# Adding the norms' squares on the vector engine before the ones-matmul

## The chip, the cores and the metric

The kernel runs on all eight cores of one Trainium2 chip. Each core computes one element of the batch by itself, with the same program and the same weights, and the cores exchange nothing. The time is that of the slowest core, in device microseconds (us). It is compared with the median of the runs of the kernel before.

## The reference

A trunk of two layers works on x (8, 2048, 1024). Each layer is: half-step SwiGLU FFN, token mixer, cross-attention into 256 memory tokens, half-step FFN. Every one of these eight sub-layers has an RMS norm ahead of it (pre-norm) and one behind it (post-norm):

```python
def rms_norm(x, g):
    xf = x.astype(jnp.float32)
    y = xf * lax.rsqrt(jnp.mean(xf * xf, axis=-1, keepdims=True) + EPS)
    return (y * g.astype(jnp.float32)).astype(x.dtype)

h = swiglu(rms_norm(x, g[0]), ...)
x = x + HALF * rms_norm(h, g[1])
h = rms_norm(x, g[2]); h = even_mixer(h, ...)   # layer 0; odd_mixer in layer 1
x = x + rms_norm(h, g[3])
h = cross_attention(rms_norm(x, g[4]), rms_norm(mem, mem_norm_g[l]), ...)
x = x + rms_norm(h, g[5])
h = swiglu(rms_norm(x, g[6]), ...)
x = x + HALF * rms_norm(h, g[7])
```

The mean runs over the 1024 channels. It is this sum of squares over the channels that the change is about.

## The kernel before

**Layout.** Channels lie on partitions: the 1024 channels are 8 chunks (c) of 128. The 2048 tokens are four blocks (tb) of 512, and a half (hf) is two blocks. X holds the residual stream (float32, 8 chunks by 2048 tokens), XN the normed input (bf16), HO the output of a sub-layer before its post-norm (float32, 8 chunks by the 1024 tokens of a half). HO2 is a second HO, used only by the second half of attention. Weights stream from memory through eight slots, issued on POOL.

**A group** is a run of matmuls into one bank of PSUM (8 banks, ps0 to ps7): 8 matmuls of 512 columns in a projection, 22 in the FFN's down projection. `k.bank()` hands out the banks in rotation and passes over those that are reserved.

**Sum over channels.** The chunks are summed over partitions by matmuls with a constant matrix (ONESM, all 1/1024), which add a chunk's squares over its 128 partitions and leave the sum on every partition. Two places do it:

- Post-norm, `HalfOut.evac(c, tb, bank)`: ACT copies the group's result, scaled by the gain, into HO (L577), squares the same bank into a small bf16 tile SQD (L580, three tiles in rotation), and two groups later PE takes that square through ONESM (`stat_mm`), eight matmuls for a block of tokens, into a bank kept reserved from chunk 0 on.
- Pre-norm, `prenorm_steps`: `sa` squares chunks 0 to 3 of X into SQP (one ACT instruction, L518), `sb_` takes them through ONESM in four matmuls and then squares chunks 4 to 7 into the same SQP (L525), `sc1` takes these through ONESM in four more, makes the reciprocal root on ACT (`rstd_from`, L463 and L465, an Ln and an Exp) and lets DVE write XN for chunks 0 to 3 (`xn_apply`, L531), `sc2` the same for 4 to 7.

**Order.** There is no scheduler: each engine executes its instructions in the order in which the Python code records them, and waits by semaphores on the keys of the tiles that it reads and writes. A key that another engine still has to read is waited for too. What belongs to a norm is recorded in between the groups of whatever follows: `run_seq(steps)` takes a list of (count, step), and a step is recorded once that many groups have gone by (`_tick`), or sooner, all steps up to it, when an operation outside the list needs a key that a step of the list writes or reads (`_check`), or when the next list begins (`need`). Before the change a ones-matmul of `evac` counts as a group too.

**After a half**, `finish` records such a list: the last ones-matmuls, then step A (or A2, two chunks of both blocks), in which DVE multiplies HO by the root (L620, L658) and DVE or POOL adds it to X (L622, L661), and then the pre-norm steps of the next sub-layer for these tokens. Behind the output projections of mixers and attention (`out_proj`), the evacuations are held back by three groups, and the second half's groups follow the first half's at once. There the list of the first half runs beside the groups of the second, and what is left of it is recorded in one go when the second half finishes; then the next sub-layer's first groups are recorded, which need all of XN of the first two blocks.

## Time and profile before

| | |
|---|---|
| median of 3 runs | 3073.16 us (3071.93 to 3591.28) |
| the profiled execution's own time | 3073.69 us |
| its span on the slowest core | 3072.1 us |
| PE busy | 2887.0 us (94%), 13124 matmuls |
| DVE busy | 1002.2 us (33%) |
| ACT busy | 1059.4 us (34%) |
| POOL busy | 627.8 us (20%) |
| spans of the eight cores | 3062.0 to 3072.1 us |
| mean granted TensorE clock of the cores | 0.970 to 0.973 |

The span goes from the first to the last instruction of the slowest core; 1.6 us of the execution lie outside it. Busy time is the union of an engine's instructions, and a busy PE may still be running at its lower clock, which is why the count of matmuls in a stretch says more than its busy share.

### The profile page before, as it was taken

The numbers are of one execution on the slowest core, as the hardware profiler recorded it, in microseconds if no ns is written. First come the engines' busy times: TensorE is split into PE (matmuls) and PEld (weight loads), VectorE is DVE, ScalarE is ACT, GpSimd is POOL, SyncE is SP. The second block draws the span as 40 slices with busy tenths as digits, with TensorE's granted clock in tenths as the row PEclk, the third lists the DMA queues.
The fourth block names the chain that finished last, engine by engine and source line by source line (L and its number), as shares of the span: only waits on it lengthen the run. The fifth ranks groups of instructions, "written<-read, shape, count | busy, mean of one in ns | idle before, by whom it ended". The sixth has DMA issues, their size and how long they took to land.

```text
span 3072.1 us, 38455 instructions; the slowest of 8 cores (3062.0 to 3072.1 us)
## 1 busy us (share of the span) xinstructions
PE 2887.0 (94%) x13124; PEld 1286.1 (42%) x13124; DVE 1002.2 (33%) x1485; ACT 1059.4 (34%) x1588; POOL 627.8 (20%) x966
## 2 busy tenths in 40 slices
PE   6999999889987889999999999998998898999997
PEld 2444444333333434444444444443443443444443
DVE  3212312242236336105105105205645427312212
ACT  4123213214764564124124124122126376213112
POOL 1114113110022122114112114112113204111121
PEclk9999999889998999999999999999999999999998
DMA  7554545353033434545555545554453622545667
GB/s 170 76 75 71 79 69 79 55 76 42 6 53 49 73 56 62 75 70 79 76 72 76 76 67 78 77 72 65 72 90 48 93 35 48 76 73 91 118 90 144
DMA packets 126173, 226.78 MB, mean 74 GB/s; under 512 B 13088, under 2 KB 24608, under 8 KB 125984
## 3 DMA queue, kind: packets, MB, share of 16 engines
q0 software_dynamic: 115376, 205.28, 45.2%
q1 hardware_dynamic: 10608, 19.03, 2.0%
q8 instruction: 112, 1.84, 0.3%
q14 instruction: 77, 0.63, 0.1%
HBM read 421.10 MB, written 8.39 MB: 140 GB/s over the span
## 4 chain that ended last, share of the span: by engine, by line
PE 81%; DVE 7%; ACT 6%; issue 3%; DMA 2%; POOL 0%; DVEq 0%; ACTq 0%; POOLq 0%; SPq 0%
PE ps L220 81%; DVE HO L620 3%; DVE XN L531 1%; DMA slot<-wflat 1%; DVE DG L797 1%; DVE X L622 1%; ACT sqp L525 1%; ACT RD L1163 0%; ACT ET L1151 0%; ACT RD L1164 0%; ACT r L463 0%; ACT L939 0%; ACT sqp L518 0%; ACT sqd L580 0%; ACT r L465 0%
## 5 line engine op out<-in xcount | busy, mean ns | idle before, releaser
L220 PE MATMUL ps<-XN,slot 128*128 128x512 bf16 x7296 | 1628.7, 384 | 45.0 <-DVE XN L531 31.7
L220 PEld LDWEIGHTS ps<-XN,slot 128*128 128x128 bf16 x7296 | 718.6, 99 | 944.5 <-issue 109.2
L321 POOL DMA_DIRECT2D slot<-wflat x800 | 425.0, 535 | 2255.9 <-PE ps L220 2216.1
L220 PE MATMUL ps<-H,slot 128*128 128x512 bf16 x2816 | 626.1, 379 | 1.5 <-DMA slot<-wflat 1.5
L748 DVE TENSOR_TENSOR H<-ps,s 128x512 bf16<-128x512 f32 x352 | 241.7, 690 | 1115.1 <-PE ps L220 1096.1
L739 ACT ACTIVATE s<-ps 128x512 f32<-128x512 f32 x352 | 209.3, 598 | 801.3 <-PE ps L220 733.9
L220 PEld LDWEIGHTS ps<-H,slot 128*128 128x128 bf16 x2816 | 275.2, 98 | 334.6 <-issue 3.6
L577 ACT ACTIVATE HO<-ps,cf_sb 128x512 f32<-128x512 f32 x256 | 176.5, 690 | 515.4 <-PE ps L220 507.9
L620 DVE TENSOR_TENSOR HO<-HO,r 128x512 f32<-128x512 f32 x192 | 194.4, 1037 | 97.4 <-ACT r L465 97.4
L531 DVE SCALAR_TENSOR_TENSOR XN<-X,cf_sb,r 128x512 bf16<-128x512 f32 x256 | 176.7, 758 | 137.6 <-ACT r L465 137.6
L622 POOL TENSOR_TENSOR X<-X,HO 128x512 f32<-128x512 f32 x104 | 153.8, 1504 | 106.7 <-DVE HO L620 102.3
L580 ACT ACTIVATE sqd<-ps 128x512 bf16<-128x512 f32 x256 | 152.4, 595 | 55.0 <-PE ps L220 55.0
L220 PE MATMUL ps<-sqp,onesm 128*128 128x512 bf16 x256 | 77.0, 430 | 55.9 <-ACT sqp L518 35.7
L220 PE MATMUL ps<-O,slot 128*128 128x512 bf16 x512 | 118.6, 379 | 0.2
L220 PE MATMUL ps<-CC,DG 128*128 128x512 bf16 x496 | 114.2, 389 | 0.0
L220 PE MATMUL ps<-sqd,onesm 128*128 128x512 bf16 (+1 forms) x272 | 97.2, 375 | 14.0 <-ACT sqd L580 14.0
L658 DVE TENSOR_TENSOR HO<-HO,r 128x512 f32<-128x512 f32 x64 | 44.9, 735 | 132.2 <-ACT r L465 132.2
L525 ACT ACTIVATE sqp<-X 128x2048 bf16<-128x2048 f32 x32 | 61.2, 1911 | 67.9 <-PE ps L220 41.8
L220 PEld LDWEIGHTS ps<-O,slot 128*128 128x128 bf16 x512 | 49.9, 98 | 60.7 <-issue 1.1
L220 PEld LDWEIGHTS ps<-CC,DG 128*128 128x128 bf16 x496 | 49.3, 99 | 61.9 <-issue 7.1
L622 DVE TENSOR_TENSOR X<-X,HO 128x512 f32<-128x512 f32 x88 | 66.0, 750 | 9.5 <-DVE HO L620 0.5
L518 ACT ACTIVATE sqp<-X 128x2048 bf16<-128x2048 f32 x32 | 61.0, 1906 | 13.7 <-POOL X L622 10.1
(99 smaller groups left out, 1349.6 us busy)
## 6 DMA issues: line engine op xcount, KB each, us to landing
slot<-wflat POOLq DMA_DIRECT2D x728, 256.0 KB, 4.5
slot<-wflat POOLq DMA_DIRECT2D x72, 192.0 KB, 3.5
X<-xT SPq DMA_DIRECT2D x8, 1024.0 KB, 24.2
yT<-X SPq DMA_DIRECT2D x4, 2048.0 KB, 11.4
M<-memT SPq DMA_DIRECT2D x2, 1024.0 KB, 7.2
cb_sb<-cb POOLq DMA_DIRECT2D x1, 224.0 KB, 9.9
cf_sb<-cf SPq DMA_DIRECT2D x1, 152.0 KB, 3.0
ALT<-alt POOLq DMA_DIRECT2D x1, 4.0 KB, 3.1
```

Of the source, the lines that this page charges most:

```text
L220: fn = (lambda e, l_=l_, r_=r_, st=st, sp=sp: e.matmul(out, lhsT=l_, rhs=r_, start=st, stop=sp))
L321: self.k.dma("pool", lambda e, dst=dst, src=src: e.dma_start(out=dst, in_=src), "w%d" % idx, reads=([("X", c, 0) for c in range(4)] if i = ...
L518: k.op("act", lambda e: e.activation(out=SQP[:, :, :], in_=X[:, 0:4, lo:hi], func=AF.Square), reads=[xk(c, tb) for c in range(4)], writes= ...
L525: k.op("act", lambda e: e.activation(out=SQP[:, :, :], in_=X[:, 4:8, lo:hi], func=AF.Square), reads=[xk(c, tb) for c in range(4, 8)], writ ...
L531: k.op("dve", lambda e, c=c, oap=oap: e.scalar_tensor_tensor(out=oap, in0=X[:, c, lo:hi], scalar=G(l, n, c), in1=R[r][:, :], op0=ALU.mult, ...
L577: k.op("act", lambda e: e.activation(out=oap, in_=P[bank][:, :], func=AF.Copy, scale=gcol), reads=[("P", bank)] + CONST, writes=okeys)
L580: k.op("act", lambda e: e.activation(out=SQD[i][:, :], in_=P[bank][:, :], func=AF.Square), reads=[("P", bank)], writes=[("SQD", i)])
L620: k.op("dve", lambda e, hap=hap: e.tensor_tensor(out=hap, in0=hap, in1=R[r][:, :], op=ALU.mult), reads=hkeys + [("R", r)], writes=hkeys)
L622: k.op(add_eng_for(tb), lambda e, hap=hap, c=c: e.tensor_tensor(out=X[:, c, lo:hi], in0=X[:, c, lo:hi], in1=hap, op=ALU.add), reads=hkeys ...
L658: k.op("dve", lambda e, hap=hap, r=r: e.tensor_tensor(out=hap, in0=hap, in1=R[r][:, :], op=ALU.mult), reads=hkeys + [("R", r)], writes=hkeys)
L739: k.op("act", lambda e, bg=bg, s=s: e.activation(out=SS[s][:, :], in_=P[bg][:, :], func=AF.Silu), reads=[("P", bg)], writes=[("S", s)])
L748: k.op("dve", lambda e, bu=bu, s=s, hap=hap: e.tensor_tensor(out=hap, in0=P[bu][:, :], in1=SS[s][:, :], op=ALU.mult), reads=[("P", bu), (" ...
```

## The change

The squares are first added up over the chunks, elementwise, by DVE, and one ones-matmul takes the sum.

- Post-norm: for chunk 0, `evac` writes the square in float32 straight into HO's own chunk 7 of these tokens (`acc`), which chunk 7's result will need only at the end. For chunks 1 to 6 ACT squares into SQD (now two tiles) and DVE adds SQD to acc. For chunk 7 DVE adds acc and SQD into a bf16 tile SQF, then ACT writes chunk 7's result into HO. One ones-matmul reads SQF. It is recorded by `finish`, so no bank is reserved before.
- Pre-norm: `add4(h)` adds the four squares of SQP in two DVE instructions, one of 1024 elements into SQT (float32), one of 512 into SQA[h] (bf16). `sb_` records add4(0) and the second square, a new step `sc0` records add4(1), and `sc1` two ones-matmuls on SQA[0] and SQA[1]. The counts in the lists are set anew: in the list of `finish` for one chunk at a time, `sb_` and `sc0` come with A(tb_, 2) and A(tb_, 5), `sc1` with A(tb_, 7), and `sc2` after it.
- The tiles take 7 KB more; the room comes from a smaller scratch area for DMA descriptors. One unused constant goes.

```diff
-    SQD = [sb("sqd%d" % i, OFF_SQ + i * 1024, [TB], BF16) for i in range(3)]
-    SQP = sb("sqp", OFF_SQ + 3 * 1024, [4, TB], BF16)
+    SQD = [sb("sqd%d" % i, OFF_SQ + i * 1024, [TB], BF16) for i in range(2)]
+    SQF = [sb("sqf%d" % i, OFF_SQ + (2 + i) * 1024, [TB], BF16) for i in range(2)]
+    SQP = sb("sqp", OFF_SQ + 4 * 1024, [4, TB], BF16)
+    SQT = sb("sqt", OFF_SQ + 8 * 1024, [2, TB], F32)
+    SQA = [sb("sqa%d" % i, OFF_SQ + (12 + i) * 1024, [TB], BF16) for i in range(2)]
...
+            def add4(h):
+                k.op("dve", lambda e: e.tensor_tensor(out=SQT[:, :, :], in0=SQP[:, 0:2, :], in1=SQP[:, 2:4, :], op=ALU.add),
+                     reads=[("SQP",)], writes=[("SQT",)])
+                k.op("dve", lambda e: e.tensor_tensor(out=SQA[h][:, :], in0=SQT[:, 0, :], in1=SQT[:, 1, :], op=ALU.add),
+                     reads=[("SQT",)], writes=[("SQA", h)])
+
             def sb_():
-                st["b"] = bnk = k.bank(reserve=True)
-                for c in range(4):
-                    k.mm(P[bnk][:, :], [(ONESM[:, :], SQP[:, c, :], [("SQP",), ("ONES",)])], bnk, start=(c == 0), stop=False)
+                add4(0)
                 k.op("act", lambda e: e.activation(out=SQP[:, :, :], in_=X[:, 4:8, lo:hi], func=AF.Square),
                      reads=[xk(c, tb) for c in range(4, 8)], writes=[("SQP",)])
+
+            def sc0():
+                add4(1)
...
             def sc1():
-                bnk = st["b"]
-                for c in range(4):
-                    k.mm(P[bnk][:, :], [(ONESM[:, :], SQP[:, c, :], [("SQP",), ("ONES",)])], bnk, start=False, stop=(c == 3))
+                bnk = k.bank(reserve=True)
+                k.mm(P[bnk][:, :], [(ONESM[:, :], SQA[h][:, :], [("SQA", h), ("ONES",)]) for h in range(2)], bnk)
                 st["r"] = rstd_from(bnk, TB, 1.0)
...
-                k.op("act", lambda e: e.activation(out=oap, in_=P[bank][:, :], func=AF.Copy, scale=gcol),
-                     reads=[("P", bank)] + CONST, writes=okeys)
-                i = k.rot("SQD", 3)
+                acc, acck = self.hoap(7, tl)
+                f = tb % 2
+
+                def scaled():
+                    k.op("act", lambda e: e.activation(out=oap, in_=P[bank][:, :], func=AF.Copy, scale=gcol),
+                         reads=[("P", bank)] + CONST, writes=okeys)
+                if c == 0:
+                    scaled()
+                    k.op("act", lambda e: e.activation(out=acc, in_=P[bank][:, :], func=AF.Square),
+                         reads=[("P", bank)], writes=acck)
+                    return
+                i = k.rot("SQD", 2)
                 k.op("act", lambda e: e.activation(out=SQD[i][:, :], in_=P[bank][:, :], func=AF.Square),
                      reads=[("P", bank)], writes=[("SQD", i)])
-                self.pend.append((tb, c, i))
-                self.stat_mm(2)
+                if c < 7:
+                    scaled()
+                    k.op("dve", lambda e: e.tensor_tensor(out=acc, in0=acc, in1=SQD[i][:, :], op=ALU.add),
+                         reads=acck + [("SQD", i)], writes=acck)
+                    return
+                k.op("dve", lambda e: e.tensor_tensor(out=SQF[f][:, :], in0=acc, in1=SQD[i][:, :], op=ALU.add),
+                     reads=acck + [("SQD", i)], writes=[("SQF", f)])
+                scaled()
+                self.pend.append((tb, f))
...
-                steps += [(0 if not steps else 1, sa), (3, sb_), (3, sc1), (1, sc2)]
+                steps += [(0 if not steps else 1, sa), (2, sb_), (3, sc0), (2, sc1), (1, sc2)]
...
-                    steps += [(1, both(A(tb_, 0), sa0)), (1, A(tb_, 1)), (1, A(tb_, 2)), (1, both(A(tb_, 3), sb0)),
-                              (1, A(tb_, 4)), (1, A(tb_, 5)), (1, both(A(tb_, 6), sc10)), (1, both(A(tb_, 7), sc20)),
-                              (2, sa1), (3, sb1), (3, sc11), (1, sc21)]
+                    steps += [(1, both(A(tb_, 0), sa0)), (1, A(tb_, 1)), (1, both(A(tb_, 2), sb0)), (1, A(tb_, 3)),
+                              (1, A(tb_, 4)), (1, both(A(tb_, 5), sc00)), (1, A(tb_, 6)), (1, both(A(tb_, 7), sc10)), (1, sc20),
+                              (1, sa1), (2, sb1), (3, sc01), (2, sc11), (1, sc21)]
...
                     steps = [(2, fin_stats), (1, A2(0)), (1, A2(2)), (1, A2(4)), (1, A2(6)),
-                             (9, sa0), (11, sb0), (3, sc10), (1, both(sc20, sa1)), (3, sb1), (3, sc11), (1, sc21)]
+                             (9, sa0), (8, sb0), (4, sc00), (2, sc10), (1, both(sc20, sa1)), (2, sb1), (3, sc01), (2, sc11),
+                             (1, sc21)]
```

Over the whole program PE has 416 matmuls fewer (512 of 512 columns with ONESM become 96). DVE has 288 additions of 512 elements more (192 in `evac` for chunks 1 to 6, 32 for chunk 7, 64 in add4) and 64 of 1024. Lines of the changed kernel are given by its own numbers below.

**ACT in the even mixer's output projection, from the first half's roots (r0, r1) to the first evacuations of the second half.** Before, each evacuation is a scaled copy into HO and a square into sqd:

```order
L463 ACTIVATE r0_56<-ps0 128x512
L465 ACTIVATE r0_56<-r0_56 128x512
L463 ACTIVATE r1_57<-ps2 128x512
L465 ACTIVATE r1_57<-r1_57 128x512
L577 ACTIVATE HO_67<-ps6,cf_sb_60 128x512
L580 ACTIVATE sqd0_52<-ps6 128x512
L577 ACTIVATE HO_67<-ps7,cf_sb_60 128x512
L580 ACTIVATE sqd1_53<-ps7 128x512
```

After:

```order
L465 ACTIVATE r0_60<-ps4 128x512
L467 ACTIVATE r0_60<-r0_60 128x512
L465 ACTIVATE r1_61<-ps5 128x512
L467 ACTIVATE r1_61<-r1_61 128x512
L590 ACTIVATE HO_70<-ps2,cf_sb_64 128x512
L594 ACTIVATE HO_70<-ps2 128x512
L590 ACTIVATE HO_70<-ps3,cf_sb_64 128x512
L594 ACTIVATE HO_70<-ps3 128x512
```

The places are the same; the square of chunk 0 (L594) now goes into HO, chunk 7, which the first half's A2 steps still read.

**DVE in attention's output projection, layer 0, where the first half's last A2 step ends and the second half's additions begin (L680 multiplies HO by the root, L683 adds to X, L602 adds a square to acc, here in HO2).** In the changed kernel:

```order
L680 TENSOR_TENSOR HO_70<-HO_70,r1_61 128x512
L680 TENSOR_TENSOR HO_70<-HO_70,r0_60 128x512
L683 TENSOR_TENSOR X_43<-X_43,HO_70 128x512
L602 TENSOR_TENSOR HO2_108<-HO2_108,sqd0_52 128x512
L602 TENSOR_TENSOR HO2_108<-HO2_108,sqd1_53 128x512
L602 TENSOR_TENSOR HO2_108<-HO2_108,sqd0_52 128x512
```

The additions stand behind all 24 instructions of the four A2 steps; before, DVE had nothing for the second half's evacuations.

**DVE in the query projections of layer 0, from the last steps A of the last block to its XN (L620/L642 HO times root, L622/L644 into X, L1078/L1101 the normed memory tokens, L531/L540 XN).** Before:

```order
L531 SCALAR_TENSOR_TENSOR XN<-X,cf_sb,r_56 128x512 x4
L620 TENSOR_TENSOR HO<-HO,r_57 128x512
L622 TENSOR_TENSOR X<-X,HO 128x512
L531 SCALAR_TENSOR_TENSOR XN<-X,cf_sb,r_56 128x512 x4
L1078 SCALAR_TENSOR_TENSOR MN<-M_107,cf_sb,r_57 128x256 x8
L531 SCALAR_TENSOR_TENSOR XN<-X,cf_sb,r_56 128x512 x8
```

After:

```order
L524 TENSOR_TENSOR sqt<-sqp 128x1024
L526 TENSOR_TENSOR sqa_59<-sqt 128x512
L642 TENSOR_TENSOR HO<-HO,r_61 128x512
L644 TENSOR_TENSOR X<-X,HO 128x512
L642 TENSOR_TENSOR HO<-HO,r_61 128x512
L644 TENSOR_TENSOR X<-X,HO 128x512
L540 SCALAR_TENSOR_TENSOR XN<-X,cf_sb,r_60 128x512 x8
L524 TENSOR_TENSOR sqt<-sqp 128x1024
L526 TENSOR_TENSOR sqa_58<-sqt 128x512
L1101 SCALAR_TENSOR_TENSOR MN<-M_110,cf_sb,r_61 128x256 x8
L524 TENSOR_TENSOR sqt<-sqp 128x1024
L526 TENSOR_TENSOR sqa_59<-sqt 128x512
```

The third block's XN moves behind the last step A, and the fourth block's two add4 enclose the eight instructions for the memory tokens; its XN follows them.

## Rows read from the trace of the kernel before

**Rows 1.** The page's first line, and part 1: busy time, share, instructions.

```profile
span 3072.1 us, 38455 instructions; the slowest of 8 cores (3062.0 to 3072.1 us)
...
PE 2887.0 (94%) x13124; PEld 1286.1 (42%) x13124; DVE 1002.2 (33%) x1485; ACT 1059.4 (34%) x1588; POOL 627.8 (20%) x966
```

**Rows 2.** Busy time by stretch of 50 us: stretch, its length, engines (instructions), PEclk, DMA, GB/s.

```profile
50.00:100.00 50.00, 50.00 (x233) 22.70 (x232) 20.05 (x30) 20.62 (x24) 7.39 (x14) 1.00 0.46 69
...
900.00:950.00 50.00, 38.72 (x159) 15.89 (x158) 32.84 (x38) 29.31 (x44) 18.87 (x19) 0.86 0.31 45
...
2100.00:2150.00 50.00, 39.52 (x167) 16.50 (x166) 42.53 (x58) 15.94 (x18) 17.83 (x21) 0.92 0.42 61
```

**Rows 3.** Groups of instructions by form: shapes, count | busy us, mean ns | idle before.

```profile
L220 PE MATMUL ps<-sqd,onesm 128*128 128x512 bf16 x256 | 92.8, 381 | 14.0 <-ACT sqd L580 14.0
...
L220 PE MATMUL ps<-sqp,onesm 128*128 128x512 bf16 x256 | 77.0, 430 | 55.9 <-ACT sqp L518 35.7 <-ACT sqp L525 16.7 <-DVE HO L620 3.5
...
L975 DVE SCALAR_TENSOR_TENSOR TT<-CV,cf_sb,TT 128x1025 f32<-128x1025 f32 x16 | 20.6, 1288 | 1.7
...
L942 DVE SCALAR_TENSOR_TENSOR gs_d<-gs_d,cf_sb,gs_sd 128x512 f32<-128x512 f32 x16 | 12.0, 752 | 90.9 <-ACT gs_sd L941 85.2 <-PE ps L220 5.7
...
L838 DVE TENSOR_TENSOR USY<-UF 128x1023 bf16<-128x1023 bf16 x4 | 2.8, 690 | 0.3
...
L525 ACT ACTIVATE sqp<-X 128x2048 bf16<-128x2048 f32 x32 | 61.2, 1911 | 67.9 <-PE ps L220 41.8 <-DVE X L622 13.2 <-POOL X L622 12.8
...
L465 ACT ACTIVATE r<-r 128x512 f32<-128x512 f32 x64 | 40.4, 632 | 5.9
```

**Rows 4.** Timeline, even mixer's output projection: start us, us, instruction, idle before.

```profile
884.67 0.81 PE L220 MATMUL ps<-sqd,onesm 128*128 128x512 bf16 x3
...
892.79 0.69 DVE L658 TENSOR_TENSOR HO<-HO,r 128x512 f32<-128x512 f32 x1 [32.57 <-ACT r L465]
...
908.39 0.71 ACT L577 ACTIVATE HO<-ps,cf_sb 128x512 f32<-128x512 f32 x1
...
909.43 0.73 ACT L577 ACTIVATE HO<-ps,cf_sb 128x512 f32<-128x512 f32 x1
...
914.32 1.58 POOL L661 TENSOR_TENSOR X<-X,HO 128x512 f32<-128x512 f32 x1 [1.29 <-DVE HO L658]
...
914.88 1.57 DVE L661 TENSOR_TENSOR X<-X,HO 128x512 f32<-128x512 f32 x1
...
941.38 0.38 PE L220 MATMUL ps<-XN,slot 128*128 128x512 bf16 x1 [0.29 <-DVE XN L531]
```

**Rows 5.** Timeline, query projections behind it.

```profile
961.23 1.03 PE L220 MATMUL ps<-sqp,onesm 128*128 128x512 bf16 x4
...
974.68 4.02 DVE L1078 SCALAR_TENSOR_TENSOR MN<-M,cf_sb,r 128x256 bf16<-128x256 f32 x8 [0.84 <-ACT r L465]
...
978.62 5.38 DVE L531 SCALAR_TENSOR_TENSOR XN<-X,cf_sb,r 128x512 bf16<-128x512 f32 x8
...
979.51 17.43 PE L220 MATMUL ps<-XN,slot 128*128 128x512 bf16 x56 [4.29 <-DVE XN L531]
```

**Rows 6.** Timeline, attention's output projection in layer 0.

```profile
1102.00 0.81 PE L220 MATMUL ps<-sqd,onesm 128*128 128x512 bf16 x3
...
1108.84 0.69 DVE L658 TENSOR_TENSOR HO<-HO,r 128x512 f32<-128x512 f32 x1 [31.00 <-ACT r L465]
...
1131.00 1.57 DVE L661 TENSOR_TENSOR X<-X,HO 128x512 f32<-128x512 f32 x1
...
1157.05 0.38 PE L220 MATMUL ps<-XN,slot 128*128 128x512 bf16 x1 [0.29 <-DVE XN L531]
```

**Rows 7.** Timeline, rows of three other places.

```profile
560.55 5.39 DVE L531 SCALAR_TENSOR_TENSOR XN<-X,cf_sb,r 128x512 bf16<-128x512 f32 x8 [7.82 <-ACT r L465]
...
1187.66 1.03 PE L220 MATMUL ps<-sqp,onesm 128*128 128x512 bf16 x4
...
2148.41 3.57 PE L220 MATMUL ps<-XN,slot 128*128 128x512 bf16 x8 [1.81 <-DVE BE L991]
```

More of the change, by code:

```diff
@@ L22 @@
 NCORES = 8
-SB_BASE = 16512
+DMA_SCRATCH = 8192
+SB_BASE = DMA_SCRATCH + 128
 SB_TOP = 229344
@@ L30 @@
 OFF_SQ = OFF_SLOTS + NSLOT * 2048
-OFF_R = OFF_SQ + 7 * 1024
+OFF_R = OFF_SQ + 14 * 1024
 OFF_S = OFF_R + 2 * 2048
@@ L39 @@
 OFF_ONES = OFF_CB + NCB * 2
-OFF_END = OFF_ONES + 256 + 256 + 512
+OFF_END = OFF_ONES + 256 + 256
 assert SB_BASE + OFF_END <= SB_TOP, (SB_BASE + OFF_END, SB_TOP)
@@ L376, in build @@
 def build(nsub=8):
-    nc = bass.Bass("TRN2", target_bir_lowering=False)
+    nc = bass.Bass("TRN2", target_bir_lowering=False, dynamic_dma_scratch_size=DMA_SCRATCH)
     xT = nc.dram_tensor("xT", [D, S], F32, kind="ExternalInput").ap()
@@ L398, in build @@
     ONES1 = sb("ones1", OFF_ONES + 256, [128], BF16)
-    ONESF = sb("onesf", OFF_ONES + 512, [128], F32)
     P = [nc.alloc_psum_tensor("ps%d" % i, [128, TB], F32) for i in range(8)]
@@ L547, in prenorm_steps @@
             keyed(sb_, [xk(c, tb) for c in range(4, 8)])
+            keyed(sc0)
             keyed(sc1, [xk(c, tb) for c in range(4)], XN((0, 4), (lo, hi))[1])
             keyed(sc2, [xk(c, tb) for c in range(4, 8)], XN((4, 8), (lo, hi))[1])
-            return sa, sb_, sc1, sc2
+            return sa, sb_, sc0, sc1, sc2
         def prenorm_chain(l, n, tbs):
@@ L554, in prenorm_chain @@
             for tb in tbs:
-                sa, sb_, sc1, sc2 = prenorm_steps(l, n, tb)
-                steps += [(0 if not steps else 1, sa), (3, sb_), (3, sc1), (1, sc2)]
+                sa, sb_, sc0, sc1, sc2 = prenorm_steps(l, n, tb)
+                steps += [(0 if not steps else 1, sa), (2, sb_), (3, sc0), (2, sc1), (1, sc2)]
             run_seq(steps)
@@ L588, in stat_mm @@
                 while len(self.pend) > keep:
-                    tb, c, i = self.pend.pop(0)
-                    if tb not in self.pst:
-                        self.pst[tb] = k.bank(reserve=True)
-                    bnk = self.pst[tb]
-                    k.mm(P[bnk][:, :], [(ONESM[:, :], SQD[i][:, :], [("SQD", i), ("ONES",)])], bnk,
-                         start=(c == 0), stop=(c == 7))
+                    tb, f = self.pend.pop(0)
+                    self.pst[tb] = bnk = k.bank(reserve=True)
+                    k.mm(P[bnk][:, :], [(ONESM[:, :], SQF[f][:, :], [("SQF", f), ("ONES",)])], bnk)
             def finish(self, nxt, hf, cpb=1):
-                fin_stats = keyed(lambda: self.stat_mm(0), [("SQD", i_) for i_ in range(3)], [])
+                fin_stats = keyed(lambda: self.stat_mm(0), [("SQF", i_) for i_ in range(2)], [])
                 ta, tb_ = self.tbs[0], self.tbs[-1]
@@ L639, in finish @@
                 elif cpb == 1:
[L640 to L644 removed]
+                    sa0, sb0, sc00, sc10, sc20 = prenorm_steps(nxt[0], nxt[1], ta)
+                    sa1, sb1, sc01, sc11, sc21 = prenorm_steps(nxt[0], nxt[1], tb_)
+                    steps += [(1, both(A(tb_, 0), sa0)), (1, A(tb_, 1)), (1, both(A(tb_, 2), sb0)), (1, A(tb_, 3)),
+                              (1, A(tb_, 4)), (1, both(A(tb_, 5), sc00)), (1, A(tb_, 6)), (1, both(A(tb_, 7), sc10)), (1, sc20),
+                              (1, sa1), (2, sb1), (3, sc01), (2, sc11), (1, sc21)]
                 else:
@@ L668, in A2 @@
                         return keyed(fn, ks, ks)
-                    sa0, sb0, sc10, sc20 = prenorm_steps(nxt[0], nxt[1], ta)
-                    sa1, sb1, sc11, sc21 = prenorm_steps(nxt[0], nxt[1], tb_)
+                    sa0, sb0, sc00, sc10, sc20 = prenorm_steps(nxt[0], nxt[1], ta)
+                    sa1, sb1, sc01, sc11, sc21 = prenorm_steps(nxt[0], nxt[1], tb_)
                     steps = [(2, fin_stats), (1, A2(0)), (1, A2(2)), (1, A2(4)), (1, A2(6)),
-                             (9, sa0), (11, sb0), (3, sc10), (1, both(sc20, sa1)), (3, sb1), (3, sc11), (1, sc21)]
+                             (9, sa0), (8, sb0), (4, sc00), (2, sc10), (1, both(sc20, sa1)), (2, sb1), (3, sc01), (2, sc11),
+                             (1, sc21)]
                 run_seq(steps)
@@ L1058, in mem_sq @@
                 map_, mk = M32(c, (0, MEM))
-                i = k.rot("SQD", 3)
+                i = k.rot("SQD", 2)
                 k.op("act", lambda e: e.activation(out=SQD[i][:, 0:MEM], in_=map_, func=AF.Square),
```

3 lines of the change are left out of this document (removed).

## The prediction

> **What bounds the kernel now.** I read the page's first two parts, then busy time by stretches, then the timeline where PE is not full. PE is busy for 94% of the span, and DVE, ACT and POOL for a third or less [rows 1]. In a full stretch PE starts 233 matmuls in 50 us, one per 0.2146 us; elsewhere it starts 159 or 167, at a granted clock of 0.86 or 0.92 [rows 2]. The reader should see two regimes. In the FFNs, the convolution and the first halves of the output projections PE never waits, and a matmul less is 0.2146 us less. At the second halves of the output projections, the query projections behind the mixers and the starts of the mixers, a chain over ACT, DVE and POOL sets when PE goes on. There a matmul less gives nothing by itself, and an instruction more on DVE costs its duration.
>
> **What is removed.** 416 ones-matmuls: 89.3 us at 0.2146. 224 are post-norm squares (seven of eight for each of 32 blocks), 192 pre-norm squares (six of eight, 32 times). Inside chain-bound stretches lie the post-norm ones of the second halves of four output projections (56), and the pre-norm ones of 22 blocks (132): two at the start, four at each mixer's output and query projections, two at each mixer's start, four around each attention's. The other 228 lie where PE is full: **-48.9 us**. For the stretches with the 188 I rebuild the chain and compare its length; their matmuls are in those lengths.
>
> **What is added, a piece.** 288 additions of 512 elements and 64 of 1024 on DVE. A 512 addition in the kernel takes 0.69 us while POOL rests (at 892.79) and 1.57 while POOL adds too (at 914.88) [rows 4]. The wide one is not in the trace. The three-operand form takes 752 ns at 512 and 1288 ns at 1025 [rows 3], so 513 elements cost 0.54 and the wide addition 0.69 + 0.53 = 1.22 us. Bounds: 0.69, the bf16 addition of 1023 elements [rows 3], and 1.29. I take 1.22, because SQT is float32, as in the 1025 row; so an add4 is 1.22 + 0.1 + 0.69 = 2.0 us. The 0.69 row of 1023 elements has bf16 on all sides. The Trainium skill ("VectorE: DVE Perf Modes", What auto-detection actually checks) says two bf16 elements go per cycle only if every tensor is 16-bit, and its fp32 formula gives 1.22; by it the sum stays, by the 0.69 row it would be some 15 us less.
>
> **Mixer output projection, second half (twice).** T is the end of the first half's last group, 884.67; the second group of the query projection ends at 941.6, T + 56.9 [rows 4]. The A2 steps start on DVE at 892.79. Four ones-matmuls and a short wait ahead of it go (1.5 us), so T + 6.6. They run 23.1 us to POOL's last addition (914.32 + 1.58) and 23.7 to DVE's last: T + 29.7 and T + 30.3. Now the new wait: the square of chunk 0 goes to HO, chunk 7, which exactly those last additions read. ACT stands at it until T + 29.7, and all evacuations are queued behind. PE fills the banks: six groups and two ones-matmuls, 6 x 1.72 + 0.4 = T + 10.7, and the seventh needs the bank of the first. It starts at T + 30.6, **a wait of 20 us** where before ACT ran its copy and square every 1.04 us all along [rows 4]. Ten groups are left, 17.2 us, and 2 us for a restart at the lower clock (eight matmuls in 3.57 us against 1.72, [rows 7]): T + 49.8. Then in one chain: last square, last addition and wide addition to 52.9, the X square of 1.91 [rows 3] to 54.9, add4 to 57.0, two ones-matmuls, Ln and Exp (0.63 each, [rows 3]) to 59.1, eight XN of 5.4 [rows 5] to 64.6; for the other block add4 (66.6), its square from 65.9 to 67.8, add4 to 69.9, ones-matmuls, Ln and Exp to 72.0, XN to 77.4, end of the group T + 77.8. So **+20.9 us, twice**. Of it 20 is the wait; the rest of the chain is as long as before, since add4 stands for four matmuls at the lower clock.
>
> **Query projections behind it (twice).** DVE is the bound here: before the last XN come the memory tokens (974.68) and XN of the fourth block at 978.62, PE goes on at 979.51 [rows 5]. After: two add4 for the third block (+3.9) delay its XN's end from 973.8 (974.68 less the 0.84 idle) to 977.7. In PE's order the ones-matmuls of that block stood at 961.23 [rows 5] and waited for ACT alone; now they wait for DVE's queue, until 969.6, and PE loses its lead. For the fourth block: add4(0) to 979.6, square to 980.9, the root of the memory tokens behind it on ACT to 982.3, eight memory instructions of 4.0 to 986.4, add4(1) to 988.4, ones, Ln, Exp 990.3, and PE goes on at 991.2: **+11.7 us, twice**.
>
> **Attention's output projection, second half (twice).** acc lies in HO2 here, so chunk 0 does not wait. But all four A2 steps stand ahead of the second half's additions on DVE. Before, T = 1102.0, A2 from 1108.84 to 1132.57, and the third group of the FFN done about 1157.9 (the last waits for XN end at 1157.05), T + 55.9 [rows 6]. After: DVE free at T + 29.0, the first additions at 29.7 and 30.4. With two SQD tiles ACT can take chunks 0 and 1 and stops at the square of chunk 2. PE has twelve groups' worth of banks, T + 21.1, waits 10 us, and starts again at T + 31.1. ACT then works off twelve evacuations at 1.04 us and a square (1.9) with two waits for chunk 7, to T + 45.9; the same tail as above gives T + 71.7: **+15.8 us, twice**.
>
> **Other places.** Even mixer's start: 3.9 us of add4 ahead of the third block's XN, and the fourth block's add4 behind the gate's multiplication; XN at 560.55 [rows 7] becomes 565.6, **+5**. Odd mixer's start, where DVE is busy for 42.5 of 50 us [rows 2]: nearly both add4 pairs count, **+7**. First FFN stage after each attention: PE reaches the ones-matmul (1187.66, [rows 7]) at 1185 and waits 2.6 us for DVE, but waits and matmuls worth 6 go, **-2.6, twice**. Start of the kernel, where add4 queues behind the first H: **+1.5**. Last stage, partly held by the weights' transfers: **+2** of the gain lost. Hidden and costed at nothing: the 112 + 16 additions in full PE stretches, under groups of 1.72 or 4.7 us; were the cover gone, each would cost 0.7.
>
> **Sum.** -48.9 + 41.8 + 23.4 + 31.6 + 5 + 7 - 5.2 + 1.5 + 2 = **+58.2 us**. On the span of 3072.1 that is 3130.3, with the 1.6 us outside it 3131.9. The profiled execution is 0.5 above the median of the runs, which I neglect: **3132 us**, 1.9% slower than the median. 2%, about what a measurement of this kernel can tell from no change, is 61.5 us, or 3134.6.
>
> **Rivals.**
> 1. The forecast's mechanism, 3110 to 3155. For it: each wait follows from one key and one order. Chance 0.56, of which 0.25 above 3134.6.
> 2. Slower still: PE lives on its lead over DVE. At the mixers' starts and in the first FFN stage after attention DVE runs up to seven groups behind PE, and PE now stops at the ones-matmul until DVE has caught up. I took 2.6 us there. If DVE is the whole lead behind, 12 us, it costs some 9 us more at four places, half of it kept: +18 to +36, about 3160. It decides if PE comes to the ones-matmul more than 5 us before DVE has done add4(1). For it: DVE's 42.5 of 50 [rows 2]. Against it: PE's own waits at 1187 are short. A part of the same: additions at 1.57 instead of 0.69 while POOL adds [rows 4]. The Trainium skill ("GPSIMD Engine Reference", Specifications) names the same contention for instructions with two SBUF inputs, which all the new ones are; the trace agrees. Chance 0.25.
> 3. The waits at attention are covered (ACT gets further than chunk 1 because DVE's steps run shorter), 3085 to 3105. Chance 0.13.
> 4. Faster: no new wait shows, because the second half's squares find HO, chunk 7, free, and all 89 us come back: 3073.7 - 89.3 = 2984. That needs 23 us of A2 steps under 10.7 us of free banks. Chance 0.04.
> 5. The change doesn't do what it says (the matmuls stay, or other tiles collide in the arena): the counts and the keys speak against it. 0.02.
>
> **Range and chances.** 3100 to 3168 holds the first, most of the second, and the bounds of the wide addition (0.69 gives 3117, 1.29 gives 3134). Faster by over 2%: 0.05. Slower by over 2%: 0.25 + 0.23 = 0.48. Within 2%: 0.47.
>
> **What would show it.** ACT's L594 idle for about 19 us in each mixer's second half, waiting for POOL's or DVE's X, and PE idle for 20 us right then; the squares L598 waiting for DVE's L602 at attention and PE 10 us; add4's wide addition at 1.22 us; PE waiting for L526 in front of the sqa matmuls; 233 matmuls in 50 us in the FFNs as before, so that these end 1 us sooner for 5 matmuls less. The prediction is wrong if L594 starts as soon as its bank is full, if DVE's queue is short where I have it long, or if the clock stays low after the long waits, which would cost up to 15 us at each of the four.

## The result, and the profile after

The changed kernel took **3210.9 us** (median of four runs, three of them 3208.8 to 3212.2) against 3073.1: a ratio of 1.0447 (95% interval 1.0424 to 1.0471). Forecast were 3132 us, a range of 3100 to 3168, and as likely "within 2%" as "slower". The direction was right, the size was not: the loss is 138 us, not 58. Executions in which the cores of one die ran at a much lower clock are left out of the ratio and of all times below.

The page's first line, and part 1, of the changed kernel, to be held against [rows 1]:

```profile
span 3207.2 us, 38558 instructions; the slowest of 8 cores (3172.8 to 3207.2 us)
...
PE 2837.8 (88%) x12708; PEld 1257.9 (39%) x12708; DVE 1277.5 (40%) x1836; ACT 1059.8 (33%) x1588; POOL 628.8 (20%) x966
```

416 matmuls fewer and 351 instructions more on DVE, as counted. But PE's share fell from 94% to 88%: the time went into waits. The spans also lie in two groups, 3207 and 3172 to 3183 us, where before all lay between 3062 and 3072. So two things are to be found: why the shorter cores lost 110 us, and why two lost 26 more.

**The 26 us.** Busy time by stretch of 50 us in an FFN of layer 1, core 1 and core 5 (the first row of each is its heading; the columns are those of [rows 2]):

```profile
core 1: us, PE busy (x) PEld busy (x) DVE busy (x) ACT busy (x) POOL busy (x), PEclk, DMA share, GB/s
...
2000.00:2050.00 50.00, 50.00 (x192) 20.74 (x191) 8.30 (x12) 7.18 (x12) 6.34 (x12) 0.81 0.44 64
...
core 5: us, PE busy (x) PEld busy (x) DVE busy (x) ACT busy (x) POOL busy (x), PEclk, DMA share, GB/s
...
2000.00:2050.00 50.00, 50.00 (x233) 22.66 (x232) 9.68 (x14) 8.96 (x15) 7.91 (x15) 1.00 0.49 74
```

PE is wholly busy on both, but core 1 starts 192 matmuls where core 5 starts 233. Its granted clock is 0.81, which is neither of the two levels (1.2 and 2.4 GHz, granted 0.5 and 1.00). On cores 0 and 1 this holds for 159 us, from 1953 to 2112, in this trace on no other core. I therefore read the change on core 5, whose clock is 1.00 there.

**The 110 us.** I numbered all matmuls but those with ONESM (12596 in both kernels) and compared when each starts, core 5 after against the profiled core 3 before. The growth of the difference over a place is what the place lost. "Mixers' output projection" goes from the end of the first half to the second group of the query projections, as in the forecast; the others likewise. Us, both layers together:

```
place                                 forecast  changed  post only  pre only
start of the kernel                        1.5      2.1        0.0       3.7
mixers' starts (2)                        12.0     19.3       -1.6      18.0
mixers' output projections (2)            41.8     42.2       33.9       4.5
query projections behind them (2)         23.4     23.4       -0.8      23.6
attention's output projections (2)        31.6     34.1       22.5       5.2
first FFN half behind attention (2)       -5.2     16.0       -1.5      15.5
18 groups into the next FFN half (4)       0.0     15.6        0.0      16.2
all else                                 -46.9    -44.8      -38.6      -9.9
sum                                       58.2    107.9       13.9      76.8
```

The last two columns are from experiments below. These sums are one core against another and hold to some us only: the six cores of the changed kernel without 0.81 end at 100 to 111 us in place of the 107.9. Five rows came out within 3 us of the forecast. Three are wrong: both FFN rows, which lost 31.6 us against a forecast gain of 5.2, and the mixers' starts, 7.3 us more than forecast.

What is seen where the forecast held: timeline of the even mixer's output projection on core 5, to be held against [rows 4].

```profile
913.72 1.58 POOL L683 TENSOR_TENSOR X<-X,HO 128x512 f32<-128x512 f32 x1 [1.30 <-DVE HO L680]
...
914.28 1.56 DVE L683 TENSOR_TENSOR X<-X,HO 128x512 f32<-128x512 f32 x1
...
915.39 0.60 ACT L594 ACTIVATE HO<-ps 128x512 f32<-128x512 f32 x1 [20.21 <-POOL X L683]
...
916.23 1.86 PE L221 MATMUL ps<-YA,slot 128*128 128x512 bf16 x4 [19.68 <-ACT HO L594]
```

The square of chunk 0 stands idle for 20.21 us until POOL's last addition to X has read HO, chunk 7, and PE for 19.68 us behind it (forecast: 20). In attention, where acc lies in HO2, it is the third square into SQD:

```profile
1161.71 1.28 DVE L602 TENSOR_TENSOR HO<-HO,sqd 128x512 f32<-128x512 f32 x2
...
1162.48 0.60 ACT L598 ACTIVATE sqd<-ps 128x512 bf16<-128x512 f32 x1 [19.03 <-DVE HO L602]
...
1163.81 6.37 PE L221 MATMUL ps<-O,slot 128*128 128x512 bf16 x19 [9.76 <-ACT HO L590]
```

DVE's first additions come behind the last A2 step, and PE waits 9.76 us (forecast: 10).

What is seen where it failed: 18 groups into the second half of the first FFN, core 5.

```profile
300.08 1.64 DVE L642 TENSOR_TENSOR HO<-HO,r 128x512 f32<-128x512 f32 x2
301.65 2.28 DVE L524 TENSOR_TENSOR sqt<-sqp 128x1024 f32<-128x1024 bf16 x1
...
301.96 0.38 PE L221 MATMUL ps<-sqa,onesm 128*128 128x512 bf16 x1
...
304.03 1.56 DVE L526 TENSOR_TENSOR sqa<-sqt 128x512 bf16<-128x512 f32 x1
...
305.74 0.59 PE L221 MATMUL ps<-sqa,onesm 128*128 128x512 bf16 x1 [3.41 <-DVE sqa L526]
306.12 6.21 PE L221 MATMUL ps<-XN,slot 128*128 128x512 bf16 x16
```

POOL adds to X for the steps A just then, so add4 takes 2.28 + 1.56 = 3.8 us and not 2.0. PE comes to the second ones-matmul and stands for 3.41 us, and the next 16 matmuls take 6.21 us instead of 3.4, at the lower clock. Behind attention it is worse, since there DVE multiplies and adds the second block by itself:

```profile
1228.02 0.69 DVE L526 TENSOR_TENSOR sqa<-sqt 128x512 bf16<-128x512 f32 x1
...
1228.86 0.58 PE L221 MATMUL ps<-sqa,onesm 128*128 128x512 bf16 x1 [6.02 <-DVE sqa L526]
...
1234.02 1.22 DVE L524 TENSOR_TENSOR sqt<-sqp 128x1024 f32<-128x1024 bf16 x1
1235.34 0.69 DVE L526 TENSOR_TENSOR sqa<-sqt 128x512 bf16<-128x512 f32 x1
...
1236.18 0.59 PE L221 MATMUL ps<-sqa,onesm 128*128 128x512 bf16 x1 [6.73 <-DVE sqa L526]
```

Two waits, 12.8 us, where the forecast had one of 2.6. In the list of groups by form of the changed kernel, which is that of its slowest core, all waits at these 64 matmuls are one row:

```profile
L221 PE MATMUL ps<-sqa,onesm 128*128 128x512 bf16 x64 | 30.5, 492 | 204.0 <-DVE sqa L526 203.8
```

204 us of idle time, against 55.9 before the 256 matmuls that they replace [rows 3].

### The profile page after: what moved, and what is told of

Same layout as the page of the kernel before. It is cut to its first block, busy times and chain, and to the rows that moved or that the text cites. A ratio compares the mean times of both kernels' runs of the same rounds, so it can differ in the third digit from the quotient of the medians.

```text
span 3207.2 us, 38558 instructions; the slowest of 8 cores (3172.8 to 3207.2 us)
## 1 busy us (share of the span) xinstructions
PE 2837.8 (88%) x12708; PEld 1257.9 (39%) x12708; DVE 1277.5 (40%) x1836; ACT 1059.8 (33%) x1588; POOL 628.8 (20%) x966
## 4 chain that ended last, share of the span: by engine, by line
PE 74%; DVE 14%; ACT 6%; issue 4%; DMA 1%; POOL 0%; DVEq 0%; ACTq 0%; POOLq 0%; SPq 0%
PE ps L221 74%; DVE HO L642 3%; DVE sqt L524 2%; DVE XN L540 2%; DVE X L683 1%; DVE HO L680 1%; DMA slot<-wflat 1%; DVE X L644 1%; DVE DG L820 1%; ACT sqp L531 1%; DVE sqa L526 1%; ACT r L465 1%; ACT sqd L598 1%; ACT r L467 1%; ACT RD L1186 0%
## 5 line engine op out<-in xcount | busy, mean ns | idle before, releaser
L221 PE MATMUL ps<-XN,slot 128*128 128x512 bf16 x7296 | 1659.1, 390 | 24.9 <-DVE XN L540 21.1
L221 PEld LDWEIGHTS ps<-XN,slot 128*128 128x128 bf16 x7296 | 727.6, 100 | 945.2 <-issue 176.7
L221 PE MATMUL ps<-H,slot 128*128 128x512 bf16 x2816 | 612.3, 380 | 0.0
L602 DVE TENSOR_TENSOR HO<-HO,sqd 128x512 f32<-128x512 f32 x192 | 132.8, 692 | 540.6 <-ACT sqd L598 540.6
L598 ACT ACTIVATE sqd<-ps 128x512 bf16<-128x512 f32 x224 | 137.4, 613 | 455.7 <-PE ps L221 417.0
L221 PE MATMUL ps<-sqa,onesm 128*128 128x512 bf16 x64 | 30.5, 492 | 204.0 <-DVE sqa L526 203.8
L642 DVE TENSOR_TENSOR HO<-HO,r 128x512 f32<-128x512 f32 x192 | 190.1, 1015 | 35.1 <-ACT r L467 35.1
L540 DVE SCALAR_TENSOR_TENSOR XN<-X,cf_sb,r 128x512 bf16<-128x512 f32 x256 | 174.8, 753 | 68.3 <-ACT r L467 67.8
L644 POOL TENSOR_TENSOR X<-X,HO 128x512 f32<-128x512 f32 x104 | 154.4, 1508 | 122.8 <-DVE HO L642 115.9
L531 ACT ACTIVATE sqp<-X 128x2048 bf16<-128x2048 f32 x32 | 61.2, 1912 | 128.1 <-DVE sqt L524 128.1
L524 DVE TENSOR_TENSOR sqt<-sqp 128x1024 f32<-128x1024 bf16 x64 | 81.2, 1268 | 26.5 <-ACT sqp L531 15.2
L221 PE MATMUL ps<-YO,slot 128*128 128x512 bf16 x256 | 57.5, 387 | 18.6 <-ACT HO L594 18.6
## 6 DMA issues: line engine op xcount, KB each, us to landing
yT<-X SPq DMA_DIRECT2D x4, 2048.0 KB, 10.6
```

The lines of the kernel that those rows point to most:

```text
L221: fn = (lambda e, l_=l_, r_=r_, st=st, sp=sp: e.matmul(out, lhsT=l_, rhs=r_, start=st, stop=sp))
L524: k.op("dve", lambda e: e.tensor_tensor(out=SQT[:, :, :], in0=SQP[:, 0:2, :], in1=SQP[:, 2:4, :], op=ALU.add), reads=[("SQP",)], writes=[( ...
L531: k.op("act", lambda e: e.activation(out=SQP[:, :, :], in_=X[:, 4:8, lo:hi], func=AF.Square), reads=[xk(c, tb) for c in range(4, 8)], writ ...
L540: k.op("dve", lambda e, c=c, oap=oap: e.scalar_tensor_tensor(out=oap, in0=X[:, c, lo:hi], scalar=G(l, n, c), in1=R[r][:, :], op0=ALU.mult, ...
L598: k.op("act", lambda e: e.activation(out=SQD[i][:, :], in_=P[bank][:, :], func=AF.Square), reads=[("P", bank)], writes=[("SQD", i)])
L602: k.op("dve", lambda e: e.tensor_tensor(out=acc, in0=acc, in1=SQD[i][:, :], op=ALU.add), reads=acck + [("SQD", i)], writes=acck)
```

## The experiments

The theory, **W**: the loss is PE's waits, for DVE at the ones-matmuls and for the buffers of the post-norm squares (HO, chunk 7, and the two SQD tiles), each to be had back at its place. Its core, **O**, is that PE stops at a ones-matmul recorded before DVE's queue can have reached add4. The rival from e5 on, **D**: DVE has too much to do at these places, and whoever moves a wait only moves it. Times of experiments are compared with runs of the kernel before on the same chip, 3072 to 3075 us.

**e1_scratch.** The change also halves the scratch area for DMA descriptors. That part alone, in the kernel before:

```diff
-SB_BASE = 16512
+DMA_SCRATCH = 8192
+SB_BASE = DMA_SCRATCH + 128
```

> The kernel before with the smaller scratch area for DMA descriptors alone (all else as before). Theory W (the loss is PE's waits for DVE at the ones-matmuls and for the square in HO, chunk 7): 3073 us, no difference. Rival S (part of the loss is the halved scratch, which makes the issue of the weights' transfers on POOL slower): over 3085 us, with weight loads later and PE waiting for slots.

3072.9 us against 3072.5, ratio 0.9993 (0.9971 to 1.0016). Rival S is out.

**e2_post_only** and **e3_pre_only.** Each keeps one part of the change and has the other as before.

```diff
 # e2: prenorm_steps as before
-                add4(0)
+                for c in range(4):
+                    k.mm(P[bnk][:, :], [(ONESM[:, :], SQP[:, c, :], ...
 # e3: evac and stat_mm as before
-                    k.op("dve", ... tensor_tensor(out=acc, in0=acc, in1=SQD[i][:, :], op=ALU.add), ...
+                self.pend.append((tb, c, i))
+                self.stat_mm(2)
```

> The changed kernel with the pre-norm squares as before (four ones-matmuls on SQP twice, no add4); only the post-norm part of the change stays. Theory W: it loses the two waits of 20 us and two of 10 us in the second halves of the output projections, about 66 us with the restarts, and gains 224 matmuls of 0.2146 us, 48 us: about 3090 us. No PE wait of over 3 us at the starts of the FFN halves. Rival P (the post-norm additions, by loading DVE, also cause the waits elsewhere): over 3120 us, with the waits at the FFN halves and mixers' starts still there.

> The changed kernel with the post-norm squares as before (eight ones-matmuls on SQD a block, additions L602 and L605 gone); only the pre-norm part (add4) stays. Theory W: if the parts add up, 110 us (the undisturbed cores' loss) less the 17 us of the post-norm part, about 3165 us, and PE waits for L526 of 150 to 200 us in all. Rival P: under 3130 us, since DVE is freed of the 224 additions and add4 comes in time.

Post only 3092.4 us (ratio 1.0060, 1.0038 to 1.0082), pre only 3151 us (1.0243, 1.0172 to 1.0314). The table shows the split by place: the waits in the FFNs, at the mixers' starts and in the query projections belong to the pre-norm part alone and are as long without the post-norm additions. Rival P is out. W had expected 3165 us of the second; it is 14 less. The parts add up to 13.9 + 76.8 = 90.7 of 107.9 us. More than half of what is missing lies at the output projections, 56.4 + 9.7 = 66.1 of 76.3 us. That add4 stands there behind late additions is a guess that no run separates. Core 5 of e2 also has two stretches of 10.6 us at a granted 0.81 in just these places (from 920 and from 2353 us), worth up to 4 us, so what is missing there may be more.

**e4_ffn_post.** The kernel before with the new evacuation in the FFNs alone.

```diff
             def evac(self, c, tb, bank):
+                if self.half:
+                    return self.evac_new(c, tb, bank)
```

> The kernel before with the post-norm part of the change in the FFNs' down projections alone (16 blocks, 112 matmuls fewer); output projections and all pre-norms as before. Theory W: the groups of 22 matmuls (4.7 us) cover a square, a copy and an addition, so PE never waits, and 112 x 0.2146 = 24 us come back: 3049 us. Rival C (fewer matmuls, but the list of steps behind each half starts later and something at its end waits): 3055 to 3073 us.

3046.0 us, ratio 0.9900 (0.9848 to 0.9952). Core 5 gains 3.02 us in each FFN half, which is about 14 x 0.2146 = 3.00, and the 16 ones-matmuls wait once, 1.9 us, at the end of the kernel. The kernel gained 26.5 us, where 112 x 0.2146 is 24. Under groups of 4.7 us the additions are free.

**e5_own_acc.** The changed kernel with acc in a tile of its own in the mixers.

```diff
-                acc, acck = self.hoap(7, tl)
+                acc, acck = ACC(tb % 2, (0, TB)) if self.n == 3 else self.hoap(7, tl)
```

> The changed kernel, but in the two mixers' output projections acc lies in a tile of its own (room that the convolution has left) instead of HO, chunk 7. Numbers are for the cores that keep their clock (3181 us in the changed kernel). Theory W: the 19 us wait at the square of chunk 0 goes, but ACT then stops at the square of chunk 3 (two SQD tiles, additions behind the A2 steps on DVE), as in attention, where PE waits 9.8 us: 2 x 10 us come back, 3161. Rival F (the key alone is the cause): both waits go wholly, 3140. Rival D (DVE's queue is the cause anyway): no change, 3178 to 3184.

3182 us; the slowest core's span in the profile is 3180.8. Timeline of core 5 in the even mixer:

```profile
898.57 0.59 ACT L595 ACTIVATE ACC<-ps 128x512 f32<-128x512 f32 x1
...
920.06 0.60 ACT L599 ACTIVATE sqd<-ps 128x512 bf16<-128x512 f32 x1 [16.65 <-DVE ACC L603]
...
921.48 1.87 PE L221 MATMUL ps<-YA,slot 128*128 128x512 bf16 x4 [11.07 <-ACT HO L591]
```

The square of chunk 0 no longer waits. But ACT now stops at a square into SQD until DVE has come to its additions, and PE behind it for 11.07 us, as in attention. The mixers' output projections lost 30.5 us instead of 42.2: 11.7 us came back, of 20 expected. The rest, as I read the timelines, goes to ACT, which has stopped longer and works off more evacuations at 1.05 us each while PE waits for banks or for the end of the chain. By place the key was worth 6 us a mixer, not the 20 us that its wait is long. Rival F is out, and rival D, which expected nothing, is wrong by place.

Rival D's time came true, but by the clock. Of the 11.7 us only 6 are left at the end of core 5's trace. 3.7 are lost in the convolution of layer 0, where e7 and e9 lose 3.5 and 3.2 as well though no edit touches it. Core 5 there, the changed kernel and then this one:

```profile
650.00:870.00 220.00, 198.10 (x862) 83.62 (x861) 60.04 (x164) 113.03 (x154) 18.48 (x35) 0.95 0.31 46
...
650.00:870.00 220.00, 199.15 (x845) 83.40 (x843) 58.86 (x162) 110.03 (x148) 17.72 (x34) 0.93 0.29 45
```

The mean granted clock is 0.93 instead of 0.95, and PE starts 17 matmuls fewer, which is 3.6 us at 0.2146. (e7 and e9 have 846 and 847 matmuls at 0.93 in a stretch of the same length.) And the clock stands at 0.81 in short stretches, such as this one on core 5 in an FFN:

```profile
1245.00:1259.00 14.00, 14.00 (x55) 5.82 (x54) 7.11 (x11) 7.46 (x10) 2.11 (x4) 0.81 0.43 60
```

55 matmuls start where 65 would at 1.00. The records of the clock have 39 us of this on core 5 and 76 us on cores 2 and 3, which are the slowest; at 0.19 of their length that is up to 7 and 14 us (an estimate). So the slowest core's span doesn't show what the key is worth.

**e6_late_ones.** The changed kernel with one step recorded eight groups later.

```diff
-  (1, A(tb_, 6)), (1, both(A(tb_, 7), sc10)), (1, sc20),
+  (1, A(tb_, 6)), (1, A(tb_, 7)),
+  (0 if hf == 1 and nxt[1] in (2, 4) else 8, sc10), (1, sc20),
```

> The changed kernel with one count changed: in the lists behind the FFN halves and behind attention's second half, the step with the ones-matmuls of the first block is recorded eight groups later (13.7 us), except where a mixer or the query projections follow. The work is the same. Theory O (PE stops at the ones-matmul since it is recorded before DVE's queue can have finished add4; XN is not needed for long after): PE's waits of 3.4 us at four places and of 6.0 + 6.7 us at two go, with their restarts, 35 us in all: 3146 on the cores that keep their clock. Rival D (DVE has more work there than fits, so the wait only moves): under 10 us gained, with waits at the later ones-matmuls or at XN.

3149 us (3146.7 to 3150.0), ratio 1.0239 (1.0210 to 1.0269). PE at the same place as above, core 5:

```profile
291.83 23.69 PE L221 MATMUL ps<-XN,slot 128*128 128x512 bf16 x109
315.36 0.59 PE L221 MATMUL ps<-sqa,onesm 128*128 128x512 bf16 x2
315.79 4.48 PE L221 MATMUL ps<-XN,slot 128*128 128x512 bf16 x20
```

and behind attention:

```profile
1237.41 3.61 PE L221 MATMUL ps<-XN,slot 128*128 128x512 bf16 x16 [1.61 <-DVE H L772]
1240.86 0.59 PE L221 MATMUL ps<-sqa,onesm 128*128 128x512 bf16 x2
```

The two ones-matmuls run back to back with no wait. The four places in the FFN halves go from +15.6 to -6.6 us, the two behind attention from +16.0 to -4.8: 43 us by place. There DVE is short for a moment (PE waits 1.4 to 1.6 us for the product H, three times), and that is all that is left of D. Theory O holds: with the same additions on the same engine, one count gives back 43 us at its places. At the end of core 5's trace 35 are left. 3.7 are lost in the convolution as in e5, and 39 us of this core stand at 0.81 too. That the end meets the expected 35 so well is luck in part.

**e7_bf16_sqt.** The changed kernel with SQT in bf16, so that the wide addition is bf16 on all sides; the sum is rounded once more.

```diff
-    SQT = sb("sqt", OFF_SQ + 8 * 1024, [2, TB], F32)
+    SQT = sb("sqt", OFF_SQ + 8 * 1024, [2, TB], BF16)
```

> The changed kernel with SQT as a bf16 tile (the sum of four squares is rounded to bf16 once more on its way). Theory L (the length of add4 on DVE is what PE waits for): the wide addition falls from 1.27 to about 0.7 us, the narrow one from 0.69 to 0.4, and where add4 is in the chain (some 22 blocks, two each) 0.8 us each come back: 35 us, 3146 on the cores that keep their clock. Rival O (what stands ahead of add4 in DVE's queue is what PE waits for): 10 to 20 us.

3151.5 us, ratio 1.0256 (1.0206 to 1.0306). The wide addition (into SQT) and the narrow one (into SQA) in the changed kernel on core 5 (ns, min/median/max):

```profile
L524 DVE TENSOR_TENSOR sqt<-sqp x64: 1207/1218/2283, 12.1 to 2735.0; 128x1024 f32<-128x1024 bf16 x64
L526 DVE TENSOR_TENSOR sqa<-sqt x64: 691/692/1578, 13.4 to 2736.3; 128x512 bf16<-128x512 f32 x64
```

and in this one:

```profile
L524 DVE TENSOR_TENSOR sqt<-sqp x64: 676/685/1755, 13.1 to 2700.0; 128x1024 bf16<-128x1024 bf16 x64
L526 DVE TENSOR_TENSOR sqa<-sqt x64: 424/426/1400, 13.9 to 2700.8; 128x512 bf16<-128x512 bf16 x64
```

0.8 us less for each add4, and 35 us less at the end of core 5's trace, spread over all places of the pre-norm. Rival O, with 10 to 20 us, is out as a full account of the wait. So length counts as well as order: a wait that e6 takes away whole, this one shortens.

**e8_ffn_and_late_pre.** e4 and beside it add4 with the late ones-matmuls for 12 blocks.

```diff
+                elif cpb == 1 and not (hf == 1 and nxt[1] in (2, 4)):
+                    sa0, sb0, sc00, sc10, sc20 = prenorm_steps(nxt[0], nxt[1], ta, True)
+                    ...
+                              (1, A(tb_, 4)), (1, both(A(tb_, 5), sc00)), (1, A(tb_, 6)), (1, A(tb_, 7)), (8, sc10), (1, sc20),
+                              (1, sa1), (3, sb1), (4, sc01), (4, sc11), (1, sc21)]
```

> The version of the FFNs' post-norms (3046 us) and beside it add4 with late ones-matmuls for the 12 blocks whose XN has time (first halves of the first FFN of each layer, second FFN of layer 0, attention's second halves). Theory O: 72 matmuls fewer and no new wait: 3046 - 15 = 3031. Rival D: the additions on DVE push the steps A of the second block and the gate products, waits of 2 to 6 us come at these places: 3040 to 3070.

3031.5 and 3036.1 us, ratio 0.9866 (0.9824 to 0.9909), where O said 3031 and D 3040 to 3070.

**e9_repairs.** The changed kernel with e5, e6 and e7 together and six SQD tiles instead of two.

```diff
-    SQD = [sb(... ) for i in range(2)]
+    SQD = [sb(... ) for i in range(6)]
-                i = k.rot("SQD", 2)
+                i = k.rot("SQD", 6)
```

> The changed kernel with acc of its own in the mixers, the late ones-matmuls, SQT in bf16 and six SQD tiles instead of two. Theory W (each repair takes its own waits, the rest stays: add4 in the chains of the output projections' ends, the mixers' starts and the query projections; ACT's backlog at 1.05 us a group): 3181 - 11 - 35 - 17 (bf16 where the late ones don't reach) - 12 (tiles) = 3106. Rival A (once no buffer is short the whole scheme pays as meant): under 3070.

3084.7 us, ratio 1.0041 (1.0026 to 1.0055), 21 less than expected (some of them are e6's, whose places give 43 us and not the 35 put in the sum): all of the changed kernel's loss but 11 us is gone, and it still isn't faster than before. Timeline of core 5, even mixer:

```profile
906.45 5.50 DVE L603 TENSOR_TENSOR ACC<-ACC,sqd 128x512 f32<-128x512 f32 x9
...
907.22 0.60 ACT L599 ACTIVATE sqd<-ps 128x512 bf16<-128x512 f32 x1 [10.90 <-DVE ACC L603]
...
918.65 0.43 DVE L527 TENSOR_TENSOR sqa<-sqt 128x512 bf16<-128x512 bf16 x1
...
919.33 0.58 PE L221 MATMUL ps<-sqa,onesm 128*128 128x512 bf16 x1 [14.86 <-DVE sqa L527]
```

PE doesn't stop inside the second half any more. It stops behind it, for 14.86 us at the first ones-matmul: ACT still stands 10.90 us behind DVE's A2 steps, and the chain ends when it ends. The mixers' output projections cost 16.7 us instead of 42.2, attention's 18.9 instead of 34.1, the query projections 16.6 instead of 23.4, the mixers' starts 11.7 instead of 19.3. So at these places, where DVE's queue is the chain, the scheme loses with six tiles as well (more were not tried), and its gain in the FFNs pays for that.

**e10_ffn_first_halves** and **e12_again.** e8 with the new evacuation in the first halves of the output projections too.

```diff
-                if self.half:
+                if self.half or self.tbs[0] == 0:
                     return self.evac_new(c, tb, bank)
```

> The last version (FFNs' post-norms, add4 with late ones-matmuls for 12 blocks) and beside it the post-norm additions in the first halves of the four output projections, where DVE is idle and HO, chunk 7, is free. Theory W: 56 matmuls fewer where PE is full, 12 us: 3031 - 12 = 3019. Rival Q (chunk 7's result, which waits for the addition, and SQF hold back the A2 steps, and with them the end of the second half): 3025 to 3035.

> The same kernel as in the run before (FFNs' post-norms, first halves of the output projections, add4 with late ones-matmuls for 12 blocks), for an interval: 3016 us against 3073, a ratio of 0.981. Theory W: within 3 us of it. Rival: the one undisturbed run of before was a lucky one, 3020 to 3030.

3016 and 3018 us, then 3018.7 with a ratio of **0.9816** (0.9801 to 0.9830), the fastest version of this study. The page of the last run and its groups by form:

```profile
span 3021.0 us, 38545 instructions; the slowest of 8 cores (3012.7 to 3021.0 us)
...
PE 2846.1 (94%) x12884; PEld 1266.6 (42%) x12884; DVE 1162.1 (38%) x1701; ACT 1058.6 (35%) x1588; POOL 628.6 (21%) x966
```

```profile
L526 DVE TENSOR_TENSOR sqt<-sqp 128x1024 f32<-128x1024 bf16 x24 | 32.4, 1350 | 0.0
...
L221 PE MATMUL ps<-sqf,onesm 128*128 128x512 bf16 x24 | 7.3, 379 | 1.9 <-DVE sqf L621 1.9
L221 PE MATMUL ps<-sqa,onesm 128*128 128x512 bf16 x24 | 7.1, 379 | 0.0
```

240 matmuls fewer, no wait at the 24 on sqa, and a single one of 1.9 us at the 24 on sqf. 240 x 0.2146 = 51.5 us, measured 56; the other 4 are not traced. PE's share is 94% again.

**e11_changed_again.** The changed kernel, unaltered, on another chip.

> The changed kernel as it is, on another chip. In its first runs some cores took 3181 us and others 3207, the latter with a granted clock of 0.81 for 170 us in an FFN. Theory K (the kernel causes it): 3207 to 3212 again. Rival I (it belongs to those runs): 3180 to 3184 on all cores, as with acc of its own.

3184.3 and 3187.0 us, ratio 1.0368 (1.0338 to 1.0398), all cores between 3176 and 3185 in the profiled run. Rival I: the long stretch at 0.81 and the 26 us belong to the first runs. One of these has a trace. That the others had it too, on two to four cores, is read from their spans of 3207 to 3211 us at a mean granted clock of 0.93. But 0.81 as such doesn't belong to them: stretches of 4 to 15 us of it stand in the traces of e2, e3, e5 to e8, e11 and e12 (in e5 on every core), in this run's on six cores. In one run of the kernel before, too, four cores took 3089.6 to 3094.0 us at a clock of 0.96 and the others 3066.8 to 3068.1 at 0.97. Why the first runs of the changed kernel had a long stretch, and why there, stays open.

## Why the prediction was wrong

**Right.** The counts; the two waits of 20 us and two of 10 us with their causes; the mixers' and attention's output projections, 76.3 us against 73.4; the query projections, 23.4 against 23.4; the gain where PE is full, 44.8 against 46.9; the wide addition, 1.218 us against 1.22. The price of an instruction and the rebuilt chains were good. In e11 the forecast is 54 us short, in the first runs 79. The mixers' output projections are right in sum and not in parts: "Of it 20 is the wait" can't be, since with that wait gone they still lost 30.5 of 42.2 us (e5).

**The step that failed** stands under "Other places": "First FFN stage after each attention: PE reaches the ones-matmul (1187.66, [rows 7]) at 1185 and waits 2.6 us for DVE", and "Hidden and costed at nothing" for what lies in full stretches. I looked at the second block's ones-matmul behind attention. There PE doesn't wait at all in the changed kernel (at 1253.69 on core 5). The first block's are those that PE reaches first, amid the steps A: it waits 6.0 and 6.7 us there. In the four FFN halves I took a full PE for a covered addition. The cover of an addition that nobody waits for is the groups beside it. The cover of one that PE waits for is how long before its ones-matmul it has been recorded, less all that stands ahead of it on DVE. The list had put the ones-matmul right behind the last step A, and add4 two steps ahead of it, among multiplications that wait for POOL. That cost 15.6 + 21.2 = 36.8 us (21.2 is 16.0 against a gain of 5.2), and e6 shows it to be a matter of that one count. The sum itself slips there as well: 2.6 us of wait less "waits and matmuls worth 6" is -3.4, not -2.6, twice; that makes the miss 1.6 us larger.

**A term mis-sized.** The mixers' starts, 19.3 against 12: by the trace the same thing once more, in a place that I had (PE waits 6.90 us for L526 at the even mixer's start, core 5); no run moved the count there. Of the 50 us by which core 5 missed, the three together are 44. Rival 2 had this mechanism ("PE now stops at the ones-matmul until DVE has caught up") and named two of the three places, at a chance of 0.25 and a price of 9 us each. Its condition, PE at the ones-matmul more than 5 us before DVE has done add4(1), came true with 6.7 us, and so did the size it named, "the whole lead behind, 12 us": 6.0 + 6.7. The evidence that I set against it, PE's short waits at 1187 before the change, was about ACT's square. It said nothing of DVE, on which these matmuls had not depended.

**A reading that was too broad:** "In the FFNs, the convolution and the first halves of the output projections PE never waits". In the kernel before PE is idle for 21 of the 220 us from 650 to 870, in the convolution of layer 0. No ones-matmul was taken away there, so the sum doesn't suffer.

**Not foreseen at all** were the 26 us at a granted clock of 0.81. The cause is open.
